# Both ends of a streamed expert loop put in another order: loads, buffers, bias products and the norm behind it

## The reference

```python
x = layer_norm(DEEPNORM_ALPHA * x + xa, ln2_g[l], ln2_b[l])
ff = moe_sublayer(x, ...)            # 32 experts, 4 for each token
x = layer_norm(DEEPNORM_ALPHA * x + ff, ln3_g[l], ln3_b[l])
# moe_sublayer, for each block of tokens of expert e with gates g:
act = clamped_swiglu(xb @ w_gu[e] + b_gu[e])     # 1024 -> 2 x 1024
yb = act @ w_down[e] + b_down[e]                 # 1024 -> 1024
acc = acc.at[tok].add(yb * g[:, None])
# second_block, first of its layers:
shift_m, scale_m, ... = ada_mod(c, ada_w[layer], ada_b[layer])
h = modulate(rms_norm(x, norm_gains[layer, 0]), shift_m, scale_m)
```

## Time and profile before

| | |
|---|---|
| median of 3 runs | 2228.4 us (2227.98 to 2229.61) |
| profiled execution, own time | 2227.09 us |
| span of the profile | 2225.3 us |
| TensorE busy | 2086.3 us (94%) |
| VectorE busy | 1027.2 us (46%) |
| ScalarE busy | 687.5 us (31%) |
| DMA | 652.77 MB, mean 293 GB/s |
| chain that ended last | TensorE 63%, DMA 30%, VectorE 3%, ScalarE 2% |

### The profile page before, as it was taken

One profiled execution on the slowest core, in us unless ns is written; L12 is line 12 of the kernel. 1 busy time (PEld: TensorE's weight loads), 2 busy tenths in 40 slices (PEclk: granted clock), 3 DMA queues, 4 the chain that ended last, 5 costly groups with the idle time before them and its releaser, 6 DMA issues.

```text
span 2225.3 us, 30415 instructions
## 1 busy us (share of the span) xinstructions
PE 2086.3 (94%) x12502; PEld 1403.0 (63%) x12502; DVE 1027.2 (46%) x1606; ACT 687.5 (31%) x888; POOL 0.6 (0%) x6
## 2 busy tenths in 40 slices
PE   7999999999999999999999998698899999999998
PEld 7999987853333333333333333486699888878996
DVE  6999847442322222222222222564645456546554
ACT  4334545411111111111111111363533443544333
POOL 0000000000000000000000000000000000000000
PEclk9999999999999999999999999899999999999999
DMA  9555668589999999999999999666477545444552
GB/s 320 178 186 182 218 227 301 196 365 424 429 429 429 429 429 429 429 429 428 429 428 428 429 429 416 227 212 249 144 232 253 177 154 187 152 152 138 177 181 83
DMA packets 181929, 652.77 MB, mean 293 GB/s; under 512 B 6704, under 2 KB 70192, under 8 KB 156880
## 3 DMA queue, kind: packets, MB, share of 16 engines
q1 hardware_dynamic: 181840, 651.47, 75.0%
HBM read 650.40 MB, written 1.05 MB: 293 GB/s over the span
## 4 chain that ended last, share of the span: by engine, by line
PE 63%; DMA 30%; DVE 3%; ACT 2%; issue 1%; SPq 0%; DVEq 0%; ACTq 0%
PE bank L744 31%; DMA ring<-w_down 30%; PE bank L765 13%; PE pair L1007 6%; PE bank L980 4%; PE bank L812 1%; PE pair L812 1%; PE pair L961 1%; PE bank L733 1%; DVE ring_low L1886 1%; ACT arena L1409 1%; DMA par<-params 0%; PE bank L820 0%; PE pair L788 0%; PE pair L1017 0%
## 5 line engine op out<-in xcount | busy, mean ns | idle before, releaser
L1886 DVE TENSOR_TENSOR ring_low<-ring,w_high 128x2048 fp32r<-128x2048 f32 (+1 forms) x179 | 404.9, 2267 | 297.5 <-ACT w_high L1340 296.4
L744 PE MATMUL bank<-x_high,w_high 128*128 128x256 f32 x1760 | 503.9, 286 | 15.9 <-DVE ring_low L1878 15.0
L744 PE MATMUL bank<-x_low,w_high 128*128 128x256 f32 x1760 | 499.8, 284 | 0.0
L744 PE MATMUL bank<-x_high,ring_low 128*128 128x256 f32 x1760 | 499.8, 284 | 0.0
L980 PE MATMUL bank<-ring,arena 128*64 128x512 f32 x2048 | 457.6, 595 | 17.5 <-DMA ring<-w_gu 16.7
L1340 ACT ACTIVATE w_high<-ring 128x2048 fp32r<-128x2048 f32 (+1 forms) x179 | 338.2, 1892 | 241.5 <-PE bank L744 106.8
L744 PEld LDWEIGHTS bank<-x_high,w_high 128*128 128x128 f32 x1760 | 339.3, 193 | 23.9 <-issue 23.3
L980 PEld LDWEIGHTS bank<-ring,arena 128*64 128x64 f32 x2048 | 142.1, 137 | 322.6 <-issue 268.3
L2296 DVE TENSOR_TENSOR arena<-bank,par 128x512 f32<-128x512 f32 x64 | 44.0, 687 | 648.2 <-PE bank L990 648.2
L744 PEld LDWEIGHTS bank<-x_low,w_high 128*128 128x128 f32 x1760 | 339.4, 193 | 1.0 <-issue 1.0
L744 PEld LDWEIGHTS bank<-x_high,ring_low 128*128 128x128 f32 x1760 | 339.2, 193 | 0.0
(11 more groups left out here) (310 smaller groups left out, 1863.3 us busy)
## 6 DMA issues: line engine op xcount, KB each, us to landing
ring<-w_gu SPq DMA_DIRECT2D x128, 2048.0 KB, 24.9
ring<-w_down SPq DMA_DIRECT2D x64, 2048.0 KB, 25.4
ring<-ada_w SPq DMA_DIRECT2D x24, 2048.0 KB, 9.2
ring<-ffn_w_gate_up SPq DMA_DIRECT2D x44, 1024.0 KB, 7.7
ring<-ret_w_in SPq DMA_DIRECT2D x12, 2048.0 KB, 7.8
ring<-w_in SPq DMA_DIRECT2D x10, 2048.0 KB, 8.0
ring<-w_in SPq DMA_DIRECT2D x16, 1024.0 KB, 10.6
ring<-ffn_w_down SPq DMA_DIRECT2D x8, 2048.0 KB, 7.8
```

The source lines that it names most:

```text
L744: mm = pe.matmul(acc_bank[:, ch * T:(ch + 1) * T], w[:, k, ch * P:(ch + 1) * P], xs[:, kk, :], start=kk + ch + n == 0, stop=kk == b.kc - 1 ...
L1886: V.tensor_tensor(low_part(u), raw_part(u), high_part(u).bitcast(F32), ALU.subtract).then_inc(sem("w_low"), 1)
```

## The change

- Expert tile k of a gate-up lies in the k-th slot to come free (`first_slots` = 1, 2, 3, 0), for all experts, in loads, products and waits. Behind the experts the plan's slot numbers are shifted by 2.
- One down tile of expert 0 is loaded behind the second `w_xo` tile, the other when that tile's products are done; the split attention result goes to the arena in place of slot 5. Expert 1's gate-up tiles no longer wait for the number of rounds. `c2` and `dec` are loaded behind the `w_xq` tiles, `rows_3` behind the last expert's tiles.
- Logits come ahead of ada product 11, the two last reductions go behind the gather and behind the transposes. The second half of `h_tok` is made in two steps with the selection between. All four gate-up tiles of expert 0 are taken in a row.
- `acc` starts as `ALPHA * h`. The bias products move into the last gate-up, over 128 rows (rows 32 to 127 of both operands are cleared by GpSimd), each in a PSUM bank of its own, and VectorE adds them.
- The last expert's down tiles go to slots 1 and 2 (the second one in two loads), its activation and its output to places of their own, and its steps are put between those of expert 30. The norm behind it goes half by half.

```diff
 def tile(self, parts):
-        t.slot = t.n % RING
+        t.slot = (t.n + self.shift) % RING
...
+        plan.shift = 2
...
+        last_slots = [plan.tiles[N1 + RING - 2 + k].slot for k in range(2)]
+        last_of = {plan.tiles[n].slot: n for n in range(N1)}
+        first_slots = sorted(last_of, key=last_of.get)
...
-        s_attn = split("attn", attn, x_high[:, :, :], x_low[:, :, :])
+        s_attn = split("attn", attn, split_big(2), split_big(3))
...
+                if t.n == xq[1].units[0].tile.n + 1:
+                    sp.dma_start(c2[:, 0:NC2], consts2).then_inc(sem("c2_in"), 16)
+                    sp.dma_start(dec, decay.rearrange("p (h t) -> p h t", h=RH)).then_inc(sem("c2_in"), 16)
...
+                if t.n == xo[1].units[0].tile.n:
+                    sp.wait_ge(sem("mm_done"), xq[1].units[1].done)
+                    down_tile(0, 1)
...
+                gu_tile(0, k, slot)
+                if last_of[slot] == xo[1].units[0].tile.n:
+                    sp.wait_ge(sem("mm_done"), xo[1].units[1].done)
+                    down_tile(0, 0)
+            for k, slot in enumerate(first_slots):
+                sp.wait_ge(m_tile[slot], 1)
+                gu_tile(1, k, slot)
             sp.wait_ge(sem("rounds_ready"), 1)
...
-            for k in range(2):
-                sp.wait_ge(m_tile[RING + k], rest + 1)
-                down_tile(NEXP - 1, k)
+            for k, slot in enumerate(last_slots):
+                sp.wait_ge(m_tile[slot], rest + 2)
+                part = 4 - 2 * k
+                sp.dma_start(last_ring[k][:, 0:part, :], down_rows(NEXP - 1, k)[:, 0:part, :]).then_inc(mloaded[slot], 16)
+            sp.dma_start(last_ring[1][:, 2:4, :], down_rows(NEXP - 1, 1)[:, 2:4, :]).then_inc(sem("last_rows"), 16)
+            sp.dma_start(rows_3, rows[:, 4 * D:6 * D]).then_inc(sem("rows_in"), 16)
             for t in plan.tiles[N1:]:
                 if t.n < N1 + RING:
-                    sp.wait_ge(m_tile[t.slot], n * NEXP)
+                    sp.wait_ge(m_tile[t.slot], rest + (3 if t.slot in last_slots else 2))
...
             def bias_rows(q):
-                pe.matmul(bank[2 + q % 2][:, :], gateT[0:NEXP, (q // 2) * P:(q // 2 + 1) * P],
-                          bdown[0:NEXP, (q % 2) * 512:(q % 2 + 1) * 512], start=True,
+                pe.matmul(bank[BIAS[q]][:, :], gateT[:, (q // 2) * P:(q // 2 + 1) * P],
+                          bdown[:, (q % 2) * 512:(q % 2 + 1) * 512], start=True,
...
+            gather(0, True)
+            ada_reduce(10)
+            pe.wait_ge(sem("ada_taken"), 12)
             turn_inputs(0)
+            ada_reduce(11)
+            pe.wait_ge(sem("m_xgT"), 1)
+            expert_gate_up(0, range(RING))
...
-            take_expert(rest + 1, False)
-            finish_expert(rest)
+            expert_gate_up(rest + 1, (0, 1))
+            pe.wait_ge(sem("rest_zero"), 2)
+            for q in range(4):
+                bias_rows(q)
+            expert_gate_up(rest + 1, (2, 3))
+            pe.wait_ge(sem("b_acc"), 4)
+            turn_gates(rest)
+            down_proj(rest, (0,))
             turn_halves(rest + 1)
+            down_proj(rest, (1,))
+            turn_gates(rest + 1, bank[0])
+            down_last(rest + 1, 0)
             scatter(rest)
+            down_last(rest + 1, 1)
             pe.wait_ge(sem("m_acc"), rest * 4 + 8)
-            finish_expert(rest + 1)
             scatter(rest + 1)
...
             gates_in(rest)
+            sigmoids(rest + 1)
             outputs_in(rest)
+            ready_roots()
+            act.wait_ge(sem("m_scatter"), rest * 4 + 4)
+            gates_in(rest + 1, bank[0])
+            act.wait_ge(m_tile[last_slots[1]], rest + 3)
+            nc.scalar.activation(y_s, bank[1][:, :], ACT.Copy).then_inc(sem("m_ys"), 1)
             high_until(units_of(aq[0])[0])
-            high_until(units_of(aq[0])[1])
             for i in range(TT):
                 root(i, 0)
-            turn_rms(t_h[0], "h0", True)
+                sum_squares(i)
+                rms_root(i, True)
+            turn_rms(t_h[0], "h0", units_of(aq[0])[1])
...
-            affine(1, t_2.src, rows_2, h_tok).then_inc(sem("h_tok"), 1)
+            V.tensor_tensor(h_tok[:, 1, :], t_2.src[:, 1, :], rows_2[:, 0:D], ALU.mult).then_inc(sem("h_gain"), 1)
...
             select(0)
-            modulation(0)
+            V.tensor_tensor(h_tok[:, 1, :], h_tok[:, 1, :], rows_2[:, D:2 * D], ALU.add).then_inc(sem("h_tok"), 1)
...
             for i in range(TT):
+                for o in range(2):
+                    q = 2 * i + o
+                    dve.wait_ge(sem("m_scatter"), rest * 4 + (q + 5))
+                    V.tensor_tensor(acc[:, i, f], acc[:, i, f], bank[4 + q][:, :], ALU.add).then_inc(sem("m_acc"), 1)
+                    measure(i, o, acc)
+                    if q == 2:
+                        scale_diag(t_h[0], 0)
+                spread(i)
...
-            for i in range(TT):
-                scale_diag(t_h[0], i)
-            for i in range(TT):
-                turn_out(t_h[0], i)
+            turn_out(t_h[0], 0)
+            scale_diag(t_h[0], 1)
+            low_until(units_of(aq[0])[0])
+            turn_out(t_h[0], 1)
```

More of the change, by code:

```diff
@@ L936, in _, with logits @@
             turn(t_2)
-            ada_reduce(10)
-            ada_product(11)
-            wait_evac_all(pe, [turn_2])
-            pe.wait_ge(sem("router_in"), 32)
-            for i in range(TT):
+            def logits(i):
+                for g in turn_2.groups[2 * i:2 * i + 2]:
+                    wait_evac(pe, g)
                 for k in range(DC):
@@ L972, in expert_gate_up @@
             def expert_gate_up(it, tiles):
[L974 removed]
+                for n in tiles:
+                    t = first_slots[n]
                     pe.wait_ge(mloaded[t], (it + 1) * 16)
                     for j in range(2):
[L977 removed]
+                        k = 2 * n + j
                         for b in range(2):
@@ L1009, in down_proj, with down_last @@
                     mm.then_inc(m_tile[RING + t], 1)
+            def down_last(e, t):
+                s = last_slots[t]
+                pe.wait_ge(sem("m_act"), e * 2 + (1 + t))
+                for j in range(4):
+                    if j == 0:
+                        pe.wait_ge(mloaded[s], (e + 2) * 16)
+                    elif t and j == 2:
+                        pe.wait_ge(sem("last_rows"), 16)
+                    k = 4 * t + j
+                    for o in range(2):
+                        mm = pe.matmul(bank[1][64 * o:64 * o + 64, :], last_actT[:, k, :],
+                                       last_ring[t][:, j, 512 * o:512 * o + 512], start=k == 0, stop=k == DC - 1)
+                mm.then_inc(m_tile[s], 1)
             def scatter(e):
@@ L2622, in _ @@
             G.memset(cv_pad[:, :, 0:TAPS_B - 1], 0.0).then_inc(sem("pads_zero"), 1)
+            pool.wait_ge(sem("cvb_step"), TAPS_B * DC)
+            pool.wait_ge(sem("x_split"), s_attn[2])
+            for rows in (slice(NEXP, 2 * NEXP), slice(2 * NEXP, P)):
+                G.memset(bdown[rows, :], 0.0)
+                G.memset(gateT[rows, :], 0.0).then_inc(sem("rest_zero"), 1)
 def _columns(v):
```

175 lines of the change are left out of this document (79 added, 96 removed).

## The result

The changed kernel took 2216.8 us in the median of five runs (2211.18 to 2219.59), the kernel before beside it 2227.98 (2224.37 to 2229.61): a ratio of 0.9944 [0.9934, 0.9954], 12.5 us of gain by the ratio. It is faster, as forecast, and the median lies 2.2 us above the predicted 2214.6. The spread, 8.4 us against 5.2 for the kernel before, is a finding of its own, to which most of the experiments go. The profiled execution is the slowest of the five: 2219.59 us around a span of 2217.8.

What follows compares the result with a forecast made beforehand. Between stream start and last tile the kernel was taken as bound by DMA bytes, with gains only at the ends: 5.9 + 8.7 - 0.8 = 13.8 us, giving 2214.6 us; own range 2212 to 2217, 8 in 10 for 2210 to 2220.

Steps and rivals of the forecast that it cites:

- start, up to P: Up to the loads of expert 30's down tiles: fewer bytes less a dry queue, 5.9 us won.
- The end: Last expert's down tiles load without waiting, steps interleaved with expert 30's: first addition 8.7 us earlier.
- T: When expert 30's last down tile has landed and its products start; first addition forecast 16.0 us later.
- The norm: First addition to the next layer's first product, done by halves: 20.8 us instead of 20.0, 0.8 later.
- The bytes: 4.39 MB taken out of the stream ahead of expert 1: 10.4 us if the queue has work.
- The hole: DMA queue dry from 478.0 to 482.5 us before expert 1's stream, taking 4.5 of 10.4 us.
- the first tile is done a quarter of 14.2 us later: Expert 0's first gate-up tile used up at 480.75 us, freeing the buffer for the next load.
- G: Start of expert 0's gate-up products on TensorE: forecast 477.2 us, before 480.18.
- the first rival: Smaller hole near 480 us, through full clock or a lossless restart: 2212.8 us, both together 2211; chance 0.13.
- the second (less won): Short work before the first gate-up costs more, or the first attention tile lands late: up to 2220 us; chance 0.17.
- The restart: An empty DMA queue does not start at full speed near 480 us: 1.8 us lost, taken once.
- Nothing behind the first layer's products is changed: Behind the first layer's products only buffer numbers differ, so 0 us was forecast there.

Runs made afterwards that it cites:

- bias variant: The change with bias products over the 32 real rows and without the four GpSimd clears: 2215.62 us, ratio 0.9943 against the kernel before.
- the change again: The unchanged changed kernel timed and profiled once more beside the kernel before: 2213.89 us, ratio 0.9931.
- both moves and the fill: The change with the second weights split later, ada reductions behind half of the first gate-up, and one dummy matmul ahead of the gather: 2212.32 us, ratio 0.9928.
- the end alone: The kernel before with only the change's end part (last expert's down tiles, interleaved steps, norm by halves): 2221.24 us, ratio 0.9966.
- the start alone: The change with last expert and norm as in the kernel before, bias products still in the last gate-up: 2220.23 us, ratio 0.9964.

## Why the prediction was right, and where it was not

The change was profiled twice, and the bias variant counts as a third look, since its start, end and norm are the change's own. Microseconds won against the profile of before, by step (P to addition was 55.3 there, addition to product 20.05, product to the span's end 789.34):

| step | forecast | change | again | bias variant |
|---|---|---|---|---|
| start, up to P | 5.9 | 0.2 | 3.4 | 6.8 |
| P to first addition | 8.7 | 9.0 | 9.1 | 8.2 |
| addition to first product | -0.8 | -0.4 | -0.4 | -0.4 |
| first product to the end | 0 | -1.3 | -1.5 | -1.6 |
| sum | 13.8 | 7.5 | 10.5 | 13.0 |

**The end** was right in mechanism and size. The first addition came 15.9 us behind T, forecast 16.0; alone the end gave 8.0 us, forecast 7.9. The 8.2 in the last column is TensorE at its own limit: there the stream was so early that the down products of the last expert followed gate-up and transposes with no wait for a DMA.

**The norm** was forecast at 20.8 and took 20.4. The first weights, whose split was forecast to end at T + 19.5, began it at 1408.59 and took 1.91, T + 19.6, and the root didn't wait for them. The weights' split on the chain was named, and moving it gave 1.8 of its 1.9.

**The bytes** stood nearly as forecast: worth 9.6 us by the last column (925.8 against 916.2) where 10.4 was forecast, if the queue has work, and none where it is dry. Bytes put back into the hole cost nothing, all of them cost 4.7.

**The hole** is the term that was mis-sized. The step that failed is "the first tile is done a quarter of 14.2 us later": it took the clock to be back when the gate-up begins, as in the profile of before. In the first two profiles of the change it was not, or not for long. SP's request for the next tile shows it, in the change, the change again and the bias variant:

```profile
485.56 0.33 SPq L634 DMA_DIRECT2D ring<-w_gu  x1
```

```profile
482.82 0.33 SPq L634 DMA_DIRECT2D ring<-w_gu  x1
```

```profile
479.31 0.33 SPq L634 DMA_DIRECT2D ring<-w_gu  x1
```

That is 5.7, 5.3 and 3.6 us behind G, forecast 3.55, and the queue was dry for 8.2, 6.5 and 2.8 us, forecast 4.5. G itself, forecast 42.6 us behind R, was 43.9, 43.0 and 40.8. In the first profile the front was late as well, R 1.4 us behind that of before. So the first rival (a smaller hole at full clock) and the second (less won) were both met, by the same start in different executions; they should have been one distribution, not two alternatives. Ten runs of the change in two groups have a median of 2214.3, range 2211.2 to 2219.6, close to the forecast's own range and its first two rivals. That the median came within 2.2 us of the forecast is in part luck: against the kernel before beside it the change won 11.2 us in one group and 15.7 in the other, forecast 13.8, and in the profiles what was left out (below) and a better norm and end set off one another.

**The restart** of an empty queue was taken at 1.8 us. In the bias variant the request falls at 479.31, and half-microsecond windows show nothing moved until 480.0, then 164 to 262 GB/s until 482.0:

```profile
479.50:480.00 0.50, 0.50 (x6) 0.19 (x4) 0.00 (x0) 0.00 (x0) 0.00 (x0) 1.00 0.00 0
480.00:480.50 0.50, 0.50 (x6) 0.21 (x4) 0.00 (x0) 0.00 (x0) 0.00 (x0) 1.00 1.37 262
480.50:481.00 0.50, 0.50 (x6) 0.17 (x4) 0.00 (x0) 0.00 (x0) 0.00 (x0) 1.00 0.78 164
```

That is 0.7 us of nothing and 1.0 lost of the next 2.0, 1.7 in all, with the second request 3.4 us behind the first. The prediction set 0 against it, from its reading of the Trainium skill ("DMA: Bandwidth & Descriptors", Anatomy of one DMA), whose section is on DMAs issued from GpSimd; these are issued by SyncE, and for them the rows decide. In the sum on a second dry queue the 19 us should be 18.5 by its own rows; nothing hangs on it.

**What was left out.** "Nothing behind the first layer's products is changed" was wrong by 1.3 to 1.6 us. The windows of the change where the next layer begins:

```profile
1424.00:1428.00 4.00, 0.84 (x4) 0.87 (x5) 2.65 (x6) 3.91 (x8) 0.00 (x0) 0.76 0.00 1
1428.00:1432.00 4.00, 4.00 (x21) 4.00 (x21) 4.00 (x3) 1.33 (x1) 0.00 (x0) 0.50 0.00 0
```

TensorE waited 4.06 us for ScalarE ahead of its first product (1427.16), and its clock fell to the lower level in that wait, so the 24 first products took 5.46 us; before, they took 3.11 at full clock. Whether the wait brings the fall is not shown, and the variants speak against it as the whole cause: with the split moved the wait is 2.27 us and the first products start at full clock, but it fell behind them all the same, and with both moves and the fill the wait is 0.70 us and the 24 products took 5.35 at the lower level:

```profile
1420.00:1424.00 4.00, 3.30 (x16) 3.26 (x16) 3.80 (x9) 3.12 (x4) 0.00 (x0) 0.50 0.00 0
```

Over all 14 profiles this last step took 787.0 to 790.9 us (789.34 before), though nothing was meant to differ in it but buffer numbers and, in some variants, when a weight is split. No run here explains that spread.

Open: why the kernel with the end alone reached P 2.5 us late in its profile (3.5 against R), and why the kernel before stands at 925.3 in the last column and the end alone at 927.7, where 916.2 and 10.4 us of bytes would be 926.6. What decides when the clock falls and returns between 462 and 484 was not found; that the executions differ, was. Of the prediction's signs of being wrong, G above 480 all but came true in the first profile (479.85).

## What to carry to other kernels

Find the one number that an end-to-end time hangs on (here front plus dry time of the DMA queue), and measure it in every profile: it told apart in one look what medians of five with a spread of 8 us could not. Where a stream has a hole, as here near 480 us, bytes put into it are free, and taking more bytes out of its front would only deepen it: the gain is bytes less hole, and the hole hangs on how soon the first buffer is used up. If that first use falls into a stretch where TensorE's granted clock changes, cost it at both levels and give the range accordingly, though one profile shows only one of them. And before a narrow spread of five times is taken as an effect, time the same kernel again.

## What was not expected of the hardware

- The clock between 462 and 484 us differed from profile to profile of the same start: low from 467 to 484 in the change, from 464 to 474 and again around 478 to 481 in the change again, from 465 to 468 in the bias variant. With it the queue was dry for anything from 2.8 to 8.2 us.
- In the start alone it fell at 462 while TensorE was busy, 1.5 us into the logits' 128x32 products, and stayed low over 6.00 of 6.00 busy us (granted clock 0.51). Ahead of them TensorE had been idle for 0.48 and 0.28 us.
- A 2 MB load asked for from an empty queue moved nothing for some 0.7 us and 164 to 262 GB/s in the next 2, where a full queue moves 424 (bias variant).
- A 128x512 fp32 matmul over 128 rows and one over 32 rows took nearly the same, 592 and 587 ns a record.
- A 128x512 fp32 dummy matmul took 0.94 us at full clock, two records of 0.47, in two variants.
